# Two transformer blocks on one core: block 2's attention, norms, output projection and router as one program block, token tile 0 ahead

## The reference, cut to what matters

```python
def second_block(x, ...):
    for l in range(DEPTH):                                   # 2
        xn = rms_norm_2(x, norm1_g[l])
        x = x + mixing_sublayer(xn, w_in[l], ...)
        xn = rms_norm_2(x, norm2_g[l])
        x = x + peer_ffn(xn, peer_wq[l], peer_keys[l], peer_u[l], peer_v[l])

def mixing_sublayer(...):
    # z = xn @ w_in; 6 heads of stick-breaking attention (softplus, suffix sums, exp),
    # 6 heads of mLSTM (weights exp(row maximum - column)), 4 groups of spatial gating;
    # each of the 16 heads is normed by its own mean square, then y @ w_out

def peer_ffn(xn, wq, sub_keys, u_tab, v_tab):
    q = (xt @ wq).reshape(t, PEER_HEADS, 2, PEER_SUBDIM)     # 8 heads, 2 x 128
    scores = einsum('thcd,hcnd->thcn', q, sub_keys)          # 128 keys a side
    # top 16 a side, top 16 of the 256 sums: idx, gate = softmax
    act = einsum('td,thkd->thk', xb, u_tab[ib])              # 16384 experts
    y = einsum('thk,thkd->td', gelu(act) * gb, v_tab[ib])
```

## Time and profile before

| | us |
|---|---|
| median of 3 runs | 2563.07 |
| profiled execution, its own time | 2566.87 |
| its span, first to last instruction | 2565.1 |
| TensorE busy | 2124.0 (83%) |
| VectorE busy | 1801.2 (70%) |
| ScalarE busy | 821.5 (32%) |
| GpSimd busy | 707.3 (28%) |
| gathers moved | 536.90 MB, 50.7% of the 16 DMA engines' span |
| all other loads and stores | 163.53 MB, 18.0% |

### The profile page before, as it was taken

One profiled execution on the slowest core, in us unless ns is written; L12 is line 12 of the kernel. 1 busy time (PEld: TensorE's weight loads), 2 busy tenths in 40 slices (PEclk: granted clock), 3 DMA queues, 4 the chain that ended last, 5 costly groups with the idle time before them and its releaser, 6 DMA issues. The chain is left out here.

```text
span 2565.1 us, 27636 instructions
## 1 busy us (share of the span) xinstructions
PE 2124.0 (83%) x8423; PEld 1362.4 (53%) x8428; DVE 1801.2 (70%) x4273; ACT 821.5 (32%) x1968; POOL 707.3 (28%) x669
## 2 busy tenths in 40 slices
PE   8689998789978877997877887788779877788777
...
GB/s 221 66 158 150 194 107 149 39 92 178 189 102 201 85 91 247 379 411 421 421 421 421 421 421 421 321 158 96 91 252 377 409 422 421 421 421 421 421 421 286
DMA packets 138667, 701.79 MB, mean 274 GB/s; under 512 B 14392, under 2 KB 38200, under 8 KB 66616
## 3 DMA queue, kind: packets, MB, share of 16 engines
q0 software_dynamic: 73728, 536.90, 50.7%
q1 hardware_dynamic: 64824, 163.53, 18.0%
...
HBM read 699.34 MB, written 1.05 MB: 273 GB/s over the span
## 5 line engine op out<-in xcount | busy, mean ns | idle before, releaser
L2097 PE MATMUL bank<-ARENA 128*128 128x512 f32 x2048 | 997.8, 635 | 242.4 <-DVE ARENA L2253 242.1
L2097 PEld LDWEIGHTS bank<-ARENA 128*128 128x128 f32 x2048 | 389.4, 200 | 841.7 <-DVE ARENA L2253 462.9
L2241 DVE CUSTOM_DVE_ANT_0 ARENA<-ARENA 128x1024 f32<-128x1024 f32 x512 | 626.0, 1223 | 225.8 <-DMA ARENA<-in_uv_rows,ARENA 218.8
L2057 POOL DMA_INDIRECT ARENA<-in_uv_rows,ARENA x512 | 544.1, 1063 | 775.9 <-PE bank L2097 676.5
L158 PE MATMUL bank<-PARTS,PARTS 128*128 128x256 f32 (+3 forms) x1488 | 486.7, 327 | 47.3 <-DVE PARTS L1417 17.1
L159 PE MATMUL bank<-PARTS,PARTS 128*128 128x256 f32 (+6 forms) x1600 | 515.9, 324 | 0.0
L160 PE MATMUL bank<-PARTS,PARTS 128*128 128x256 f32 (+6 forms) x1600 | 514.8, 323 | 0.0
L2140 ACT ACTIVATE ARENA<-ARENA 128x1 f32<-128x1 f32 x512 | 103.0, 203 | 1026.1 <-DVE ARENA L2241 1026.1
L158 PEld LDWEIGHTS bank<-PARTS,PARTS 128*128 128x128 f32 x1488 | 286.8, 193 | 74.5 <-DVE PARTS L1417 21.0
L159 PEld LDWEIGHTS bank<-PARTS,PARTS 128*128 128x128 f32 (+2 forms) x1600 | 312.1, 196 | 17.6
L160 PEld LDWEIGHTS bank<-PARTS,PARTS 128*128 128x128 f32 (+2 forms) x1600 | 311.6, 196 | 18.4
(11 more groups left out here) (247 smaller groups left out, 2012.1 us busy)
## 6 DMA issues: line engine op xcount, KB each, us to landing
ARENA<-in_w_up_tiles SPq DMA_DIRECT2D x44, 1024.0 KB, 5.7
...
ARENA<-in_wq_tiles SPq DMA_DIRECT2D x16, 1024.0 KB, 10.4
...
ARENA<-in_uv_rows,ARENA POOLq DMA_INDIRECT x512, 23.0
```

Of the source, the lines that this page charges most:

```text
L2057: nc.gpsimd.indirect_dma_start(out=slot[i % SLOTS], out_offset=None, in_=table[:, :], in_offset=bass.IndirectOffsetOnAxis(ap=picked[:, t, ...
L2097: last = nc.tensor.matmul(bank[2 * t + n][:, :], diag[i % (2 * QUAD)], slot[i % SLOTS][:, D + n * 512:D + (n + 1) * 512], start=(c == 0), ...
L2241: last = v.tensor_tensor_reduce(u, u, xn[:, t, :], 1.0, 0.0, ALU.mult, ALU.add, dots[:, t, c:c + 1])
```

## The change

Blocks 2 to 5 of a layer become one block, `mixing_out`; the input projection stays a block of its own. In the new block:

- The attention heads are in five groups, each for one token tile: tile 0 with three even and three odd heads, tile 1 with two, two and two. Tile 0 computes one key block, tile 1 two. The causal mask of the mLSTM rows is added by a matmul with the identity; the column term goes into ScalarE's exp as its bias.
- Tile 0's norm of heads, output projection, norm and router come ahead; tile 1's steps stand in between, in one written order for each engine. The head norm takes sums of squares from PSUM and folds the mLSTM divisor into the scale.
- w_out (8 pieces) is loaded at the end of the input projection and stays whole in SBUF; half its low parts are subtracted on VectorE, half on GpSimd.
- Ahead of the rows stand only the queries of head 0 and head 1 for tile 0. A router step is now (head, tiles); eight of ten steps follow inside the row stretch, two of them for tile 1 alone.
- Row slots 4 to 11 lie on the ring and on w_out's high parts, so gather 4 waits for the whole output projection (`out2_done`). The query weights share four places: heads 0 to 2 are loaded when the block starts, head 3 after both norms, 4 to 7 as places come free. The ring of diagonals has 4 places.
- `sbv`, `og` and `vaug` are written straight from PSUM; the last two chunks of the input projection change places, and og's sigmoid moves there. The next layer's first pieces are loaded after row 248 is used instead of 244.

Its core (the written orders of the engines and what they are led by; the new helpers do for one group or tile what their namesakes did for all):

```diff
-in_chunks = [("rows", 0, 384, 0), ("rows", 384, 384, 384), ("rows", 2688, 268, ML_IF),
-             ("turned", 1152, 256, 0), ("turned", 1408, 256, 2), ("turned", 1664, 256, 4),
-             ("rows", 2956, 256, SG_UV + 256), ("rows", 768, 384, SB_V), ("rows", 1920, 384, ML_V),
-             ("rows", 2304, 384, ML_O)]
+in_chunks = [("rows", 0, 384, z[:, :, 0:384]), ("rows", 384, 384, z[:, :, 384:768]),
+             ("rows", 2688, 268, z[:, :, ML_IF:ML_IF + 268]),
+             ("turned", 1152, 256, 0), ("turned", 1408, 256, 2), ("turned", 1664, 256, 4),
+             ("rows", 2956, 256, z[:, :, SG_UV + 256:SG_UV + 512]), ("rows", 768, 384, sbv),
+             ("rows", 2304, 384, og), ("rows", 1920, 384, vaug[:, :, :, 0:HD])]
...
+groups = [(0, (0, 2, 4)), (0, (1, 3, 5)), (1, (0, 2)), (1, (1, 3)), (1, (4, 5))]
+N_DIAG = 4
+steps = [(0, (0,)), (1, (0,)), (2, (0, 1)), (0, (1,)), (3, (0, 1)), (1, (1,))] + [(h, (0, 1)) for h in range(4, PH)]
+step_after_row = {1: 2, 9: 3, 17: 4, 25: 5, 33: 6, 49: 7, 65: 8, 81: 9}
...
+def sp(sp):
+    load_wq(sp, 0)
+    sp.dma_start(gain_row, a["norm2_g_2"][l:l + 1, :].broadcast_to([P, D])
+                 ).then_inc(S("x_gain_loaded"), 16)
+    sp.dma_start(arena(KEYS_AT, NSET * NKEY), a["keys_t"][l, :, :]).then_inc(S("keys_loaded"), 16)
+    sp.dma_start(base, a["layer_base"][l, :, :]).then_inc(S("base_loaded"), 16)
+    load_wq(sp, 1)
+    load_wq(sp, 2)
+    sp.wait_ge(S("x_xn"), NT)
+    load_wq(sp, 3)
+    for h in range(4, PH):
+        sp.wait_ge(S("q_filled"), step_of[1, h - 4] + 1)
+        load_wq(sp, h)
+    if next_loads:
+        sp.wait_ge(S("row_used"), 248)
+        next_loads(sp, 0, PIECES)
...
+mask(0)
+mask(1)
+y_root(0)
+mask(2)
+low(8)
+low(9)
+mask(3)
+for n in range(10, 16):
+    low(n)
+x_root(0)
+mask(4)
+y_root(1)
+for i, (t, c) in enumerate(rows):
+    if i == 0:
+        pool.wait_ge(S("sb_values"), N_GROUPS)
+        pool.wait_ge(S("ml_values"), N_GROUPS)
+    if i == 4:
+        x_root(1)
+        pool.wait_ge(S("out2_done"), 2 * NT)
+    if i % TOPK == 0:
+        pool.wait_ge(S("picked_ready"), i // TOPK + 1)
+    if i >= SLOTS:
+        pool.wait_ge(S("row_used"), i - SLOTS + 1)
+    nc.gpsimd.indirect_dma_start(
+        out=slot[i % SLOTS], out_offset=None, in_=table[:, :],
+        in_offset=bass.IndirectOffsetOnAxis(ap=picked[:, t, c:c + 1], axis=0)
+    ).then_inc(row_loaded[i % SLOTS], 16)
...
+def values(to, n, j, w, v):
+    t, heads = groups[j]
+    for i, h in enumerate(heads):
+        for kb in range(t + 1):
+            last = mm(to[:, h * n:(h + 1) * n], block(w, j, i, kb), v(kb, h), start=(kb == 0),
+                      stop=(kb == t), skip_group_check=True)
+    return last
...
+sb_scores(0)
+ml_rows(0)
+ml_rows(1)
+ml_scores(0)
+gates()
+keep_busy(8)
+suffix_sums(0)
+suffix_sums(1)
+ml_values(0)
+ml_values(1)
+sb_values(0)
+sb_values(1)
+sb_scores(2)
+ml_rows(2)
+ml_rows(3)
+turn_y(0)
+out(0, 0)
+suffix_sums(2)
+suffix_sums(3)
+ml_scores(2)
+out(0, 1)
+ml_values(2)
+ml_values(3)
+sb_values(2)
+sb_values(3)
+sb_scores(4)
+ml_rows(4)
+turn_x(0)
+ml_scores(4)
+queries(0)
+suffix_sums(4)
+ml_values(4)
+sb_values(4)
+turn_y(1)
+key_scores(0)
+out(1, 0)
+out(1, 1)
+queries(1)
+key_scores(1)
+turn_x(1)
+for i in range(len(rows)):
+    add_row(i)
+    if i in step_after_row:
+        queries(step_after_row[i])
+    if i - 4 in step_after_row:
+        key_scores(step_after_row[i - 4])
...
+high(0, 2)
+magnitudes(0, 1)
+logs(0, 1)
+high(2, 5)
+ml_weight(0)
+ml_weight(1)
+sb_weight(0)
+sb_weight(1)
+high(5, 8)
+y_squares(0)
+magnitudes(2, 3)
+ml_weight(2)
+ml_weight(3)
+logs(2, 3)
+high(8, 10)
+y_high(0)
+high(10, 16)
+sb_weight(2)
+sb_weight(3)
+x_squares(0)
+magnitudes(4)
+ml_weight(4)
+logs(4)
+take_x(0)
+take_queries(0)
+sb_weight(4)
+y_squares(1)
+y_high(1)
+take_scores(0)
+gate_exp(0)
+take_queries(1)
+x_squares(1)
+take_scores(1)
+take_x(1)
+gate_exp(1)
+for i in range(len(rows)):
+    gelu(i)
+    if i - 4 in step_after_row:
+        take_queries(step_after_row[i - 4])
+    if i - 7 in step_after_row:
+        take_scores(step_after_row[i - 7])
+    u = i // TOPK + 1
+    if i % TOPK == 1 and AHEAD <= u < len(units):
+        gate_exp(u)
...
+def diagonal(i):
+    t, c = rows[i]
+    if i % TOPK == 0:
+        normalise(i // TOPK)
+    dve.wait_ge(S("gelu_ready"), i + 1)
+    if i >= N_DIAG:
+        dve.wait_ge(S("row_used"), i - N_DIAG + 1)
+    v.tensor_scalar(diag[i % N_DIAG], ident, gelu_dots[:, t, c:c + 1], gate[:, t, c:c + 1],
+                    ALU.mult, ALU.mult).then_inc(S("diagonal_ready"), 1)
...
+scaled(0)
+scaled(1)
+gated()
+low(0, 2)
+softplus(0)
+softplus(1)
+ml_probs(0)
+ml_probs(1)
+sb_arg(0)
+sb_arg(1)
+low(2, 5)
+scaled(2)
+scaled(3)
+low(5, 8)
+y_sums(0)
+softplus(2)
+softplus(3)
+y_scaled(0)
+y_low(0)
+sb_arg(2)
+sb_arg(3)
+ml_probs(2)
+ml_probs(3)
+add_mixed(0)
+scaled(4)
+normed(0)
+take_x(0)
+softplus(4)
+ml_probs(4)
+sb_arg(4)
+y_sums(1)
+y_scaled(1)
+y_low(1)
+first_choice(0)
+second_choice(0)
+numbers(0)
+add_mixed(1)
+normed(1)
+first_choice(1)
+second_choice(1)
+take_x(1)
+numbers(1)
+for i in range(len(rows)):
+    row_dots(i)
+    if i >= 1:
+        diagonal(i - 1)
+    u = i // TOPK + AHEAD
+    if i % TOPK == 11 and u < len(units):
+        first_choice(u)
+    if i % TOPK == 15 and u < len(units):
+        second_choice(u)
+    if i % TOPK == 3 and AHEAD <= u - 1 < len(units):
+        numbers(u - 1)
```

More of the change, by code:

```diff
@@ L49 @@
 NF = FF // P
-MLQK, MLQK_W = 1152, 768
-SB_Q, SB_K, SB_V = 0, 384, 768
-ML_V, ML_O, ML_IF, SG_UV = 1152, 1536, 1920, 1932
-IN2 = 3212
-Z2 = IN2 - MLQK_W
+ML_IF, SG_UV = 768, 780
+Z2 = 1292
 NH6 = 6
@@ L1676, in _ @@
                         first.load(sp, PIECES, first.pieces)
+                        rest_of.load_out(sp)
                     @b.gpsimd
```

1286 lines of the change are left out of this document (563 added, 723 removed).

## The result

The changed kernel took 2537.59 us (median of 5 runs, 2535.23 to 2547.08) beside 2561.56 us for the kernel before (5 runs) on the same chip: a ratio of 0.9916, with a 95% interval of 0.989 to 0.9942. A second set of runs of the same two kernels gave 0.9919 (0.9894 to 0.9944). So it is faster by 24 us, and I had forecast 54: 2537.6 lies in the range of 2474 to 2552, 28.6 us above the 2509 that I gave. Less than half of the gain came. This document looks for the rest.

The account below looks back on a forecast made before the run. Bound taken: start of the gathers plus about 660 us in each layer. 2 x (-29.6 + 2.7) = -53.8 against the profiled 2566.9 gave 2513; that execution being 3.8 above the median, 2509; range 2474 to 2552.

Parts of the forecast that it names:

- The start of layer 1: Chain up to layer 1's first gather: replayed at 99.0 us, gather at 960.5, 34.6 sooner; -29.6 us after 5 for waits.
- hand-overs: Waits between engines on the chain to the first gather, unpriced in the replay: bounds 0 and 15 us, taken as 5.
- The rule that I had weighed against it: VectorE and GpSimd share an SBUF port pair under exclusive lock: 3.5 us a layer on the chain, sum then 2516.
- The wait at the fifth gather: Gather 4 waits for the output projection and tile 1's root: starts 8.1 us after the first, cost 0.
- each microsecond beyond 2 costs one: Price for delay of gather 4, whose four predecessors carry 10 us of transfer: one microsecond per microsecond beyond 2.
- Start and ramp: Expert stretch beyond its 643.4 us of gathers: 16.8 us before, bounds 0 and 16.8, taken as 7.
- rival 1: Replay too tight: waits between engines cost 15 us, the stretch's start loses 16.8 as before; 2549 us, chance 0.18.
- The query loads: Five heads' query weight loads moved into the expert stretch, 2.49 us each: 12.5 us a layer, 0 if filling gaps.
- the head steps' cover: Expert stretch: TensorE's eight router steps, 57.6 us, covered until row 85: 209 us of work against 229 of transfer.
- Layer 2's start: Chain to layer 2's first gather: same gain as in layer 1, -29.6 us.
- Rival 3: Router steps on TensorE stop the gather stream: stretch of 716.5 us per layer, 2616 us in all, chance 0.06.
- my signs: Expected profile: first gather near 966, gather 4 within 10 us, layer 2's stretch 655-672, rate near 421, TensorE below 0.97.

Follow-up runs that it names:

- the gap alone: Changed kernel without its drain and with 16 instead of 8 zero matmuls behind the gates, plus a drain behind tile 1's root, ahead of gather 4: 2530.4 us.
- the lateness: Changed kernel without its drain and with 16 instead of 8 zero matmuls behind the gates, tile 1's root moved behind the twelfth gather: 2535.04 us.
- sixteen zeros: Changed kernel without its drain, with 16 instead of 8 matmuls of zeros on TensorE behind the gates' matmuls: 2521.68 us, ratio 0.9841.

## Why the prediction was right and where it failed

**The start of layer 1: right.** The replay said 960.5 and 5 us of hand-overs; the first gather came at 965.82. That it is right to 0.3 us is in part luck, since the same head took 123.7 and 128.0 us in two other profiles. The rule that I had weighed against it left its sign too. VectorE's last two operations on the output of tile 0, beside GpSimd's low parts, and the same two on tile 1 with GpSimd idle:

```profile
897.86 1.15 DVE L2120 TENSOR_TENSOR ARENA<-ARENA,STAT 128x256 f32<-128x256 f32 x1
899.08 1.46 DVE L2122 TENSOR_TENSOR ARENA<-ARENA 128x384 f32<-128x384 f32 x1
```
```profile
949.87 0.42 DVE L2120 TENSOR_TENSOR ARENA<-ARENA,STAT 128x256 f32<-128x256 f32 x1
950.36 0.56 DVE L2122 TENSOR_TENSOR ARENA<-ARENA 128x384 f32<-128x384 f32 x1
```

1.15 and 1.46 us beside two low parts on GpSimd (L1645, 2.66 us from 897.46 on), 0.42 and 0.56 alone, for the same shapes: 1.6 us, which lie within the 5 of hand-overs. Each of the two ends 0.2 to 0.4 us behind the end of a low part, if the 2.66 us are cut in half. By the rule of the Trainium skill (SBUF — State Buffer, "SBUF: two separate sides") I had come to 3.5 a layer; these rows agree with it in kind.

**The wait at the fifth gather: the step that failed.** I put it at 0: "by the replay the root's squares come behind the queries of head 1 (3.6 us) at 967.5, so gather 4 starts at 968.6". The inputs were there 2.8 us later, at 970.3, and the root's first instruction ran as soon as the fourth gather was issued, at 970.84. What I had not priced was an instruction inside the step that I moved, the drain between its halves. Before, every root stood ahead of all gathers; the change moved one behind four of them. In the timeline of the kernel before no drain has a gather in flight, so its cost there had no row, and it wanted bounds, as the hand-overs had them: nothing, and the landing of what is in flight, 10 us of transfer. I gave it neither. (By my "each microsecond beyond 2 costs one", gather 4 at 15.5 instead of 8.1 us would have cost 5.4; the gap alone cost 3.3.) Nor did I see that the norm, the choices and the first use of a row hang on that root: "the first row is used at about 984" became 992.69 for its product with x, and its slot was free at 999.98. Measured cost: 3.3 for the gap and 4.6 for the lateness, 8 us per layer, 16 of the missing 32.

**Start and ramp: right in kind, 3 us too small.** I took 7 for 16.8. Without the drain the stretches less 643.4 and 12.5 leave 13.6 and 9.9, against 21.2 and 16.8 before: a gain of 7.6 and 6.9 per layer instead of 9.8. With the drain it was 21.7 and 17.7, that is no gain at all, and rival 1's "lose 16.8 as now", for another reason than it gave. That is 5 of the missing 32, and no run isolates their cause. A candidate stands in TensorE's rows without the drain (from 984.82 on): behind 11.35 us of waiting, at a granted clock of 0.53, its first two rows (8 passes) took 6.45 us, where I had priced a row at 1.76:

```profile
984.82 6.45 PE L1873 MATMUL bank<-ARENA 128*128 128x512 f32 x8 [11.35 <-DVE ARENA L2232]
```

**The query loads, 12.5: right**, and the head steps' cover as well. In the version without a drain and with sixteen zeros TensorE is busy all of the time from 1000 to 1080, through head steps and rows, and the rate stays at 417 to 422 GB/s.

**Layer 2's start: the term that I copied.** I took -29.6 twice. But the kernel before has no such head in layer 2: 126.99 us from the table load at 1765.36 (ScalarE's timeline of the kernel before, below) to the gather at 1892.35, where layer 1 has 131.02 from 864.13. I had read the stretches in layer 1 only.

```profile
1765.36 1.28 ACT L1889 ACT_TABLE_LOAD   x1
```
Of the 11.2 us missing, 4.0 are that, 4.9 are the changed kernel's own longer head there (with sixteen zeros it was 0.3 longer in one kernel, and 4.4 and 2.5 in two others), 1.7 lie between the last row of layer 1 and the next block (86.0 to 87.7), where I looked for nothing, and 0.6 are layer 1's too.

**The rivals.** Rival 1 (2549) had the right sign, gather 4 over 10 us behind gather 0 (15.5), and the measured 2537.6 is nearer to it than to my 2509. Its reasons were not those: hand-overs cost 5.3 and not 15. Rival 3, a stretch of 716.5, is excluded: the stream stopped for the drain, not for the head steps. Of my signs, the first gather near 966 held, and so did TensorE's share below 0.97 in the first 100 us (0.75, and 0.85 without the drain). Those of gather 4 (15.5 us behind, not 10), of the rate from 20 us on (409, not 421) and of layer 2's stretch (673.6, over 672) did not.
